# Two transformer blocks in one kernel: weight chunks prepared two ahead, totals taken by ScalarE, and the first loads of both attentions issued a stage earlier

## What is computed

```python
def first_block(x, ...):
    x = layer_norm(x, ln_in_g, ln_in_b)
    h = jnp.einsum('bsd,de->bse', x, w_in[l])
    au, av, ag, ba, bb, bg, cq, ck, cv, cg = jnp.split(h, split_points, axis=-1)
    ya = mixer_spatial_gating(au, av, ag, ..., w_spatial[l], b_spatial[l])
    yb = mixer_conformer_conv(ba, bb, bg, ...)              # 31 taps
    yc = mixer_window_attention(cq, ck, cv, cg, attn_sink[l], bias, mask)
    y = jnp.einsum('bse,ed->bsd', jnp.concatenate([ya, yb, yc], axis=-1), w_out[l])
    return layer_norm(DEEPNORM_ALPHA * x + y, post_ln_g[l], post_ln_b[l])

def second_block(x, ...):
    z = jnp.einsum('bsd,de->bse', rmsnorm(x, norm_pre_g), w_in)
    q, k, v, g_attn, c_h, c_b, c_c, g_conv = jnp.split(z, cuts, axis=-1)
    q, k = rope(q, pos), rope(k, pos)
    # attention in three patterns of stride 1, 4 and 16, mixed by their log-sum-exp
    ...
    y = jnp.einsum('bse,ed->bsd', mixed, w_out)
    return x + rmsnorm(y, norm_post_g)
```

## Time and profile before

| what | value |
|---|---|
| runs | 2424.43 us median of 3 (2419.78 to 2424.54) |
| profiled execution | 2428.2 us, span 2426.4 us |
| mean granted clock of TensorE in it | 0.938 of 2.4 GHz |
| busy | TensorE 2106.3 us, VectorE 1433.8, ScalarE 902.4, GpSimd 864.1 |

### The profile page before, as it was taken

One profiled execution on the slowest core, in us unless ns is written; L12 is line 12 of the kernel. 1 busy time (PEld: TensorE's weight loads), 2 busy tenths in 40 slices (PEclk: granted clock), 3 DMA queues, 4 the chain that ended last, 5 costly groups with the idle time before them and its releaser, 6 DMA issues.

```text
span 2426.4 us, 43240 instructions
## 1 busy us (share of the span) xinstructions
PE 2106.3 (87%) x16228; PEld 1550.3 (64%) x16228; DVE 1433.8 (59%) x3539; ACT 902.4 (37%) x1933; POOL 864.1 (36%) x956
## 2 busy tenths in 40 slices
PE   5999999785896999499999999999697878776898
PEld 3545758675785888488444444748576666665776
DVE  7514858764896544762567743121398888893421
ACT  3322222221785000332233331212297877772111
POOL 3311121262423987331112121111127666962222
PEclk9999999897898999799999999999898998897999
DMA  5441321136642232432343421211467776564443
GB/s 170 138 102 60 109 70 45 44 116 177 165 110 101 87 109 97 152 109 66 121 138 114 130 81 44 79 44 53 98 158 170 176 165 158 136 182 152 139 141 111
DMA packets 285631, 279.95 MB, mean 115 GB/s; under 512 B 39936, under 2 KB 237952, under 8 KB 285168
## 3 DMA queue, kind: packets, MB, share of 16 engines
q1 hardware_dynamic: 279200, 270.01, 38.7%
q0 software_dynamic: 1680, 5.51, 0.6%
q10 hardware_dynamic: 4544, 1.66, 0.4%
HBM read 171.22 MB, written 93.31 MB: 109 GB/s over the span
## 4 chain that ended last, share of the span: by engine, by line
PE 24%; DVE 11%; POOL 8%; issue 3%; DMA 3%; ACT 2%; SPq 2%; DVEq 0%; ACTq 0%; POOLq 0%
PE bank L172 23%; DVE s2m L2261 4%; DVE p2l L2267 3%; POOL cm L2139 1%; POOL qs L2307 1%; POOL gt L2147 1%; DMA qr<-qf 1%; DVE qf L1752 1%; POOL kept L2143 1%; POOL kept L2141 1%; SPq L1781 1%; DVE qr L1750 1%; POOL kept L2139 1%; ACT s2sh L1732 1%; POOL yo L2492 1%
## 5 line engine op out<-in xcount | busy, mean ns | idle before, releaser
L2204 PE MATMUL bank<-ident,p2r 128*128 128x128 f32 x900 | 171.9, 306 | 88.7 <-DVE p2l L2267 84.5
L172 PE MATMUL bank<-xh,w2h 128*128 128x512 f16 x640 | 245.6, 384 | 0.0
L172 PE MATMUL bank<-xl,w2h 128*128 128x512 f16 x640 | 245.3, 383 | 0.0
L172 PE MATMUL bank<-xh,w2l 128*128 128x512 f16 x640 | 245.2, 383 | 0.0
L172 PE MATMUL bank<-w1h,xh 128*128 128x256 f16 x768 | 213.0, 277 | 11.3 <-DVE s1st L902 11.3
L172 PE MATMUL bank<-w1l,xh 128*128 128x256 f16 x768 | 213.0, 277 | 0.0
L172 PE MATMUL bank<-w2h,xh 128*128 128x256 f16 x768 | 211.2, 275 | 2.0 <-issue 2.0
L172 PE MATMUL bank<-w1h,xl 128*128 128x256 f16 x768 | 212.8, 277 | 0.0
L172 PE MATMUL bank<-w2l,xh 128*128 128x256 f16 x768 | 211.1, 275 | 0.0
L172 PE MATMUL bank<-w2h,xl 128*128 128x256 f16 x768 | 211.0, 275 | 0.0
L2267 DVE SCALAR_TENSOR_TENSOR p2l<-bank,p2h 128x512 f16<-128x512 f32 (+1 forms) x288 | 164.2, 570 | 49.2 <-ACT p2h L2233 48.9
(11 more groups left out here) (339 smaller groups left out, 5635.4 us busy)
## 6 DMA issues: line engine op xcount, KB each, us to landing
scr_part<-ob SPq DMA_DIRECT2D x48, 264.0 KB, 2.7
cm<-scr_part SPq DMA_DIRECT2D x48, 264.0 KB, 5.0
w2r<-in_w_in SPq DMA_DIRECT2D x12, 1024.0 KB, 6.3
qr<-qf SPq DMA_DIRECT2D x192, 64.0 KB, 2.0
v<-scr_v SPq DMA_DIRECT2D x176, 65.0 KB, 2.2
ax<-in_x SPq DMA_DIRECT2D x16, 512.0 KB, 4.2
xr<-in_x SPq DMA_DIRECT2D x16, 512.0 KB, 4.6
bx<-scr_x SPq DMA_DIRECT2D x16, 512.0 KB, 6.4
```

The source lines that it names most:

```text
L172: ins = nc.tensor.matmul(dst, x, y, start=k == 0 and m == 0, stop=k == n - 1 and m == 2)
L2204: ins = nc.tensor.transpose(bank[:, w * hh + 128 * c:w * hh + 128 * c + 128], p[:, hh, 128 * c:128 * c + 128], ident[:])
```

## The change

Three things are done at once.

1. Chunks are prepared two ahead: in chunk c the split of c + 1, the sum, total and scale of c + 2 and the load of c + 3. In `rope_stage` and `gate_stage` the sum moves to tile 2 of a chunk, TensorE's total behind tile 3, ScalarE's scaling to tile 6, the load to tile 4, and `dve_bound` from tile 5 to tile 4. In the norm stages the first group of chunk 0 is cut in two with the total and split of chunk 1 between, and chunks 3 to 5 are begun there.
2. The total is taken out of PSUM by ScalarE (`act_total`), and GpSimd does the `max` with 1e-30.
3. Loads move a stage ahead: `w_spatial` into `conv_stage`; keys, first queries and bias of the window attention and their two memsets into `spatial_stage`; queries, keys, values and mask of the dilated attention's first pair, two memsets and the mask's rearrangement into `gate_stage`. The values go by SyncE's queue, no longer by ScalarE's. The tiles for it lie in a scope `other`, on the right side of SBUF.

```diff
@@ class Weights @@
-        def dve_total(self, n, bank):
-            dve.wait_ge(*self.added[n])
-            nc.vector.tensor_scalar(self.size[:, n, 1:2], bank[:, 0:1], 1e-30, None, ALU.max).then_inc(*self.d_t.up())
+        def act_total(self, n, bank):
+            act.wait_ge(*self.added[n])
+            nc.scalar.activation(self.size[:, n, 1:2], bank[:, 0:1], ACT.Copy).then_inc(*self.a_t.up())
...
@@ norm_stage @@
-            work.append(("group", 0, g))
+            if g > 0:
+                work.append(("group", 0, g))
+            else:
+                work += [("group", 0, 0, 0), ("total", 1), ("split", 1), ("group", 0, 0, 1)]
...
-        work += [("split", 2), ("group", 1, 3)]
+        work += [("split", 2), ("load", 3), ("group", 1, 3)]
...
-        work += [("consts",), ("load", 3), ("total", 3)]
-        work += [("group", 2, 0), ("scaled", 3)] + [("group", 2, g) for g in range(1, 4)]
+        work += [("consts",), ("total", 3), ("group", 2, 0), ("scaled", 3), ("halve", 3), ("group", 2, 1)]
+        work += [("load", 4), ("group", 2, 2), ("total", 4), ("group", 2, 3), ("scaled", 4)]
...
+    def prepare(wts, c, g):
+        items = [("halve", c + 1), ("sum", c + 2), ("total", c + 2), ("scaled", c + 2)][g:g + 1] + [("load", c + 3)] * (g == 2)
+        return [x for x in items if x[1] < len(wts.chunks)]
...
@@ spatial_stage: sp_program @@
-            nc.sync.dma_start(ws[:], A["w_spatial"][0].rearrange("h i j -> i h j")).then_inc(*w_ld.up(16))
...
+                elif item[0] == "av":
+                    sp_ahead(item[1])
                 elif item[0] == "cg":
                     i = item[1]
+                    sp_ahead(8 + i)
                     sp.wait_ge(*d_si.at(i + 1))
...
@@ rope_stage: pe_program @@
-                if m == 0:
+                if m == 1:
                     pe_bound(0)
-                if m % 8 == 1:
-                    wts.pe_total(first + x["n"] + 1, *total_bank[x["n"]])
+                if m % 8 == 3:
+                    wts.pe_total(first + x["n"] + 2, *total_bank[x["n"]])
...
     act_program
-                if m % 8 == 0:
-                    wts.act_sum(first + m // 8 + 1)
-                if m % 8 == 4:
-                    wts.act_scale(first + m // 8 + 1)
+                if m % 8 == 2:
+                    wts.act_sum(first + m // 8 + 2)
+                if m % 8 == 5:
+                    wts.act_total(first + m // 8 + 2, total_bank[m // 8][0])
+                if m % 8 == 6:
+                    wts.act_scale(first + m // 8 + 2)
...
     dve_program
-                if m % 8 == 5 and x["n"] < 5:
+                if m % 8 == 4 and x["n"] < 5:
                     dve_bound(x["n"] + 1)
...
     pool_program
-                wts.pool_scale(first + n + 1)
                 wts.pool_split(first + n + 1)
+                wts.pool_scale(first + n + 2)
...
     sp_program
-                if m % 8 == 0:
-                    wts.sp_load(first + m // 8 + 2)
+                if m % 8 == 4:
+                    wts.sp_load(first + m // 8 + 3)
                 if m >= 2:
                     sp_store(m - 2)
...
@@ gate_stage: sp_program @@
-                if m % 8 == 0:
-                    wts.sp_load(first + m // 8 + 2)
+                if m >= 12:
+                    sp_ahead(m - 12)
+                if m % 8 == 4 and first + x["n"] + 3 < len(wts.chunks):
+                    wts.sp_load(first + x["n"] + 3)
```

More of the change, by code:

```diff
@@ L244, in pool_scale @@
             pool.wait_ge(*self.total[n])
+            nc.gpsimd.tensor_scalar(total, total, 1e-30, None, ALU.max).then_inc(*self.g_u.up())
+            pool.wait_ge(*self.g_u.now())
             pool.wait_ge(*POWER)
@@ L342, in norm_stage @@
             if g == 0:
-                work += [("load", 1), ("total", 1)]
+                work.append(("load", 1))
             if g < 3:
                 work.append(("scale", g + 1))
-            if g == 0:
-                work.append(("split", 1))
             if g > 0:
@@ L686, in sp_program @@
             for item in work:
-                if item[0] == "load" and item[1] > 1:
-                    wts.sp_load(item[1] + 1)
+                if item == ("load", 2):
+                    wts.sp_load(3)
+                elif item == ("scaled", 4):
+                    wts.sp_load(5)
                 elif item[0] == "scale":
@@ L738, in conv_stage @@
             n_conv, n_ug = n_conv + (what == "conv"), n_ug + (what == "ug")
-            work.append(("load", first + n + 1))
             for g in range(4):
-                if g == 1:
-                    work.append(("total", first + n + 1))
-                if g == 2:
-                    work.append(("scaled", first + n + 1))
+                work += prepare(wts, first + n, g)
                 for kind, step in STEPS[wts.chunks[first + n]["kind"]]:
@@ L999, in spatial_stage @@
         for n in range(2):
-            if n == 0:
-                work.append(("load", first + 1))
             for g in range(4):
-                if n == 0 and g == 1:
-                    work.append(("total", first + 1))
-                if n == 0 and g == 2:
-                    work.append(("scaled", first + 1))
+                work += prepare(wts, first + n, g)
                 for step in range(2):
@@ L1818, in gate_stage @@
                     tiles.append(x)
-                    if len(tiles) % 8 == 2 and first + n + 1 < len(wts.chunks):
-                        total_bank[n] = bk.take(wts.total[first + n + 1])
+                    if len(tiles) % 8 == 4 and first + n + 2 < len(wts.chunks):
+                        total_bank[n] = bk.take(wts.total[first + n + 2])
             wts.spent[first + n] = p_mm.at(len(tiles))
@@ L1920, in gate_stage, with dilated_stage @@
         pe_program()
-    def dilated_stage(late_scope, out_dst):
+        return ready
+    def dilated_stage(late_scope, out_dst, other, q0, kk0, v0, mask2, both, ready):
         begin()
@@ L1983, in dilated_stage @@
         loading, values_next = [], pieces(1)
-        work += [("pair", 0, 4, k) for k in range(10)] + pieces(0) + [("pair", 0, 4, k) for k in range(10, 40)]
         def step(s):
```

298 lines of the change are left out of this document (165 added, 133 removed).

## The result

| | kernel before | changed kernel |
|---|---|---|
| median of runs on the same chip | 2417.74 us (7 runs, 2410.58 to 2424.54) | 2403.49 us (7 runs, 2395.85 to 2411.16) |
| ratio, 95% interval | | 0.9931 [0.9912, 0.9951] |
| profiled execution | 2428.2 us, clock 0.938 | 2403.49 us, clock 0.947 |

The kernel is faster by 0.7%, 17 us by the ratio (the two medians differ by 14), where 41 were forecast, and 2403.5 lies 3.5 us outside the range. Between the two profiled executions lie 24.7 us; 8 of them are not the change's, since the profiled execution of before, 2428.2 us, was slower than each of its kernel's seven runs.

A forecast was written before the change was run, and what follows sets the result against it. TensorE, busy 87% of the span, was taken as the bound, with gains only from its waits and lower clock. Terms -9 - 0.5 - 5.5 - 19 - 7.5 + 17 - 16.5 = -41 gave 2387.2 us profiled, 2383 median; range 2350 to 2400.

The forecast's parts named there:

- The window and the dilated stage: Starts of both attentions: VectorE's first reduction comes earlier because its loads have landed, -15.5 and -16.5 us.
- five stalls: Rotary stage, five chunks with a bound: VectorE waits at tile 4 for copies queued behind the load, 8.4 us each.
- The two rivals by which the chunks stay at 42 us: Rotary stage: the load is hidden (0.22, 2351 us), or GpSimd's lock falls into the stall (0.05, 2366 us).
- Spatial stage: Spatial stage: `w_spatial` loaded earlier gains; memsets and transfers ahead, put at +1.5 us, cost; net -5.5 us.
- the 4.9 us of `ws`: Spatial stage: TensorE's wait for `w_spatial` goes, -4.9 us, and -2 for the clock.
- The rival with its 20 us (2403): Spatial stage: transfers ahead delay it by 22 us at most, put at 20, giving 2403 us; chance 0.07.
- its sign: Spatial stage: `my` landing over 4 us later would show that transfers ahead delay the stage (2403 us).
- Window attention's start: Window attention: VectorE's first reduction earlier, -15.5 us, and -3.5 for the next 39 us with less DMA; sum -19.
- Rotary and gate start: Rotary stage and start of the gate stage together: +17 us with the longer stalls, -15 had the stall not grown.
- Norm, first block: First block's norm stage: waits for ScalarE's sum go, except the longest, with their clock: -9 us.
- conv: Conv stage: VectorE's `max` leaves a stage that ends at VectorE's pace, 0.15 us a chunk: -0.5 us.
- Norm, second block: Second block's norm stage: two waits and their clock go, 9.2 us; second group's start 2 us later; sum -7.5.

The follow-up runs named there:

- rope_behind: Changed kernel with the rotary stage's whole 1 MB load issued behind tile 4's copies `qr` instead of ahead of them: 2391.13 us, ratio 0.9881 to the kernel before.
- rope_pieces: Changed kernel with each rotary-stage load cut into four of 256 KB, behind the copies of tiles 4 to 7: 2373.82 us, ratio 0.9811 to the kernel before.
- before_load_tile4: Kernel before with only the rotary stage's load of weights moved to tile 4, for the same chunk: 2417.67 us, ratio 0.9996.
- wo_later: Changed kernel with GpSimd's split of `w_out` in the window attention waiting for VectorE's small operation: 2394.71 us, ratio 0.9891 to the kernel before.
- before_wo_later: Kernel before with GpSimd's split of `w_out` in the window attention waiting for VectorE's small operation: 2420.06 us, ratio 1.0004.
- ahead_only: Changed kernel with only the loads a stage ahead, weight chunks prepared as in the kernel before: 2397.07 us, ratio 0.9895 to the kernel before.

## Why the prediction was right in its mechanism and wrong in its size

**Right.** The sign, and both large terms of it. The window and the dilated stage began without their waits (-16.0 and -17.7 us; forecast -15.5 and -16.5). The rotary stage took back what the weights had won: the mechanism, a load behind the reduction and the copies behind the load, with five stalls (forecast 8.4, measured 7.8 on average) and TensorE's wait behind tile 3, is what the trace shows and what `rope_behind`, `rope_pieces` and `before_load_tile4` confirm. The two rivals by which the chunks stay at 42 us did not come.

**The step that failed.** *Spatial stage*: "VectorE reads what TensorE makes of them 3 to 4 us later. A transfer ahead delays them by 2 to 3 us: nearly covered. I put +1.5". It was +8.7, and here the mechanism was wanting and not only the size. I looked at the landing of `my` and at its reader. I did not look at what else SyncE waits for: the store of `mu`, whose landing went from 2.2 to up to 5.9 us with `my` queued behind it. The stretch in which it counts cost 1.8 to 6.6 us in five kernels, and 0 and 0.5 in the two that avoid it; in the changed kernel 2.9 of it are waits for `my`. And I took the 4.9 us of `ws` and their clock as won, without asking what TensorE would reach early; it met `mvl` 2 us too soon, and then ran 11.5 us at a clock of 0.85. Together these give back 4.1 to 10.5 us in five kernels with this code, where I had 1.5. How the sum splits between the two is read from traces and not shown by times. The rival with its 20 us (2403) has the right name and a size 3 times too large; that it gives the measured time is chance, and its sign, `my` landing over 4 us later, did not come (2.7 at most).

**The second.** *Window attention's start*: "I give that stretch -3.5". Instead the stage lost 0.8 after its start. Less contention did come (DMA busy 0.64 and a clock of 0.91 in its first 39 us, for 0.92 and 0.85), and with it VectorE's small operation fell on GpSimd's split, 8.8 us more in that group and 5.1 in the three groups of small operations together. `wo_later` has the stage at -22.6, even better than the -19: the sum left out the lock in this stage, at nothing, though it names it for the rotary one.

**Sizes.** Rotary and gate start +21.1 for +17: chunks of 46.9, 48.0, 48.6 and 51.6 us for 46.5 and 50, so the chunks were put 0.4 to 2.1 us too short. (The prediction's own terms for a key chunk, 42.5 + 8.4 + 2, give 52.9 and not 50.) The +21.1 is also counted from an execution that was itself 3.6 to 6.7 us slower here than three others, so the stage's cost may be up to 28. Norm, first block, -6.8 for -9, and conv +1.1 for -0.5, of which 0.6 is a longer wait for `brev` (4.5 for 3.9 us). Norm, second block, -6.5 for -7.5: the wait for `bvo` behind the cut group is 7.6 us for 4.6, where the prediction allowed 2 more.

By the table the misses are +6.3 in the spatial stage, +4.1 in the rotary, +3.8 in the window, +2.2 and +1.6 in norm and conv, +1.0 in the second norm, and -2.7 in the four others: 16.3 us, from -41 to -24.7. The other 8 us, from -24.7 to the ratio's -17, are no term at all. The prediction carried the profiled time over to a median of three that lay 6.7 us above the median of seven.

**Open.** Where the run-to-run differences of the kernel before come from. Its profiled execution is 15.5 and 15.8 us longer than those of `before_load_tile4` and `before_wo_later`, in steps of 1 to 5 us at several seams, with no wait that is much longer. The rotary stages of these two and of `ahead_only` are 3.6, 6.7 and 6.7 us shorter than that of before, which the edits don't explain. That `mvl` is the operand that TensorE meets too soon was read from the trace; no run moved it.

## What to carry to other kernels

A wait in a queue costs what stands behind it. For each load that is put into a queue, list what SyncE waits for next and what those transfers must land for; a load of 1 MB goes behind the small copies that an engine waits for, or in pieces between them, and never behind a wait for work that has only just begun.

When a wait is removed, look for the next late operand of the same engine, and for the locks between VectorE and GpSimd that its new rhythm will meet. If the same code has different lengths in several profiles, compare the mean time of small operations; one wait that sets the two engines' order was worth 0.4% here, where the large change was worth 0.7%. And look whether an added wait ever holds its engine up: one that doesn't tests nothing.

A profiled execution that is longer than most runs of its kernel makes a change look better than it is: compare it with the median of many runs before a gain is read off a difference of traces.

## What the runs showed of the hardware

An operation of 128 x 8 elements on VectorE took up to 2.34 us instead of 0.16 while GpSimd did one of 128 x 1024. Of the sixteen in the window stage, seven were hit in `rope_behind`, whose stage took 163.3 us, and none in `wo_later`, whose stage took 149.1. How hard they are hit is a matter of small shifts: `rope_pieces`, whose stage starts 0.4 us earlier than that of `rope_behind`, has 8.8 us in this group for 16.5. VectorE's operations with an operand in PSUM (0.55 and 0.61 us) kept their length beside the same GpSimd instruction in the changed kernel.

A store of 256 KB landed in 2.2 us when the transfer before it in its queue had been issued 3.5 us earlier, and in 5.9 with one of 512 KB and one of 256 KB issued in the 1.3 us ahead of it; small copies behind a load of 1 MB took 4.6 us (2.5 to 5.3), where four with no load ahead took 2.0.
